# Seven of eleven FFN chunks computed with the tokens stationary, 512 weight columns moving, and the gated values turned on TensorE

## The reference, cut to what matters

```
def swiglu(h, w_in, w_out):                 # h: 256 x 1024
    g, u = jnp.split(h @ w_in, 2, axis=-1)  # w_in: 1024 x 5632, so g and u: 256 x 2816
    return (jax.nn.silu(g) * u) @ w_out     # w_out: 2816 x 1024
```

## Time and profile before

| | us |
|---|---|
| median of 3 runs | 961.66 |
| lowest, highest | 959.19, 961.93 |
| profiled execution, its own time | 958.76 |
| its span in the trace | 957.0 |
| PE busy in the span | 915.8 (96%) |
| PE weight loads | 834.0 (87%) |
| DVE busy | 681.8 (71%) |
| ACT busy | 508.0 (53%) |
| mean granted clock of TensorE | 0.986 of 2.4 GHz |

### The profile page before, as it was taken

One profiled execution on the slowest core, in us unless ns is written; L12 is line 12 of the kernel. 1 busy time (PEld: TensorE's weight loads), 2 busy tenths in 40 slices (PEclk: granted clock), 3 DMA queues, 4 the chain that ended last, 5 costly groups with the idle time before them and its releaser, 6 DMA issues.

```text
span 957.0 us, 14577 instructions
## 1 busy us (share of the span) xinstructions
PE 915.8 (96%) x6039; PEld 834.0 (87%) x6041; DVE 681.8 (71%) x903; ACT 508.0 (53%) x800; POOL 40.6 (4%) x100
## 2 busy tenths in 40 slices
PE   4979999999999999999899999999999999999996
PEld 2879997999999988999789999998987899999974
DVE  5879876887877877998777664466797855555555
ACT  2554545744434456877574443444783744444454
POOL 2101010010000100000001000000000000000000
PEclk9889999999999999999999999999999999999998
DMA  8999772898887955675539655574236665556511
GB/s 336 375 362 323 279 253 100 281 373 304 282 294 269 317 173 176 220 265 176 177 135 363 206 177 179 188 230 141 89 133 220 206 218 192 177 182 237 197 45 44
DMA packets 125763, 212.75 MB, mean 222 GB/s; under 512 B 4753, under 2 KB 93954, under 8 KB 125698
## 3 DMA queue, kind: packets, MB, share of 16 engines
q1 hardware_dynamic: 113362, 164.63, 50.7%
q0 software_dynamic: 12336, 47.20, 14.0%
HBM read 210.75 MB, written 1.06 MB: 221 GB/s over the span
## 4 chain that ended last, share of the span: by engine, by line
PE 84%; DVE 5%; ACT 5%; DMA 4%; issue 1%; SPq 0%; DVEq 0%; ACTq 0%
PE ps L607 24%; PE ps L609 24%; PE ps L608 24%; DMA raw<-in_moba_w_qkv 3%; PE ps L658 2%; PE ps L660 2%; PE ps L666 2%; DMA ada_raw<-in_ada_w 1%; PE ps L885 1%; ACT w_hi L1113 1%; ACT w_hi L1112 1%; DVE w_lo L1562 1%; DVE w_lo L1555 1%; DVE ada_sum L1586 1%; DMA raw<-in_w_up 1%
## 5 line engine op out<-in xcount | busy, mean ns | idle before, releaser
L607 PE MATMUL ps<-h_hi,w_hi 128*128 128x256 f32 x1136 | 322.5, 284 | 0.0
L609 PE MATMUL ps<-h_hi,w_lo 128*128 128x256 f32 x1136 | 321.5, 283 | 0.0
L608 PE MATMUL ps<-h_lo,w_hi 128*128 128x256 f32 x1136 | 321.4, 283 | 0.0
L1555 DVE TENSOR_TENSOR w_lo<-raw,w_hi 128x1024 fp32r<-128x1024 f32 x145 | 177.4, 1223 | 132.8 <-ACT w_hi L1112 132.8
L1112 ACT ACTIVATE w_hi<-raw 128x1024 fp32r<-128x1024 f32 x145 | 153.1, 1056 | 219.1 <-PE ps L609 187.1
L608 PEld LDWEIGHTS ps<-h_lo,w_hi 128*128 128x128 f32 x1136 | 217.9, 192 | 1.3
L607 PEld LDWEIGHTS ps<-h_hi,w_hi 128*128 128x128 f32 x1136 | 217.9, 192 | 1.3
L609 PEld LDWEIGHTS ps<-h_hi,w_lo 128*128 128x128 f32 x1136 | 217.9, 192 | 0.0
L1562 DVE TENSOR_TENSOR w_lo<-raw,w_hi 128x1024 fp32r<-128x1024 f32 x145 | 176.7, 1219 | 0.0
L1113 ACT ACTIVATE w_hi<-raw 128x1024 fp32r<-128x1024 f32 x145 | 151.7, 1046 | 0.0
L607 PE MATMUL ps<-w_hi,o_hi 128*128 128x512 f32 x264 | 105.6, 400 | 1.1 <-DVE w_lo L1562 1.1
(11 more groups left out here) (305 smaller groups left out, 1167.4 us busy)
## 6 DMA issues: line engine op xcount, KB each, us to landing
raw<-in_ffn_w_in SPq DMA_DIRECT2D x40, 1024.0 KB, 5.3
ada_raw<-in_ada_w POOLq DMA_DIRECT2D x31, 1024.0 KB, 6.7
raw<-in_ffn_w_out SPq DMA_DIRECT2D x22, 1024.0 KB, 5.0
raw<-in_w_up SPq DMA_DIRECT2D x16, 1024.0 KB, 5.3
raw<-in_w_down SPq DMA_DIRECT2D x16, 1024.0 KB, 4.9
raw<-in_moba_w_qkv SPq DMA_DIRECT2D x12, 1024.0 KB, 10.3
raw<-in_diff_w_qkv SPq DMA_DIRECT2D x10, 1024.0 KB, 5.1
yg<-in_ada_w POOLq DMA_DIRECT2D x9, 1024.0 KB, 6.2
```

The source lines that it names most:

```text
L607: T.matmul(out_ap, hi_s, hi_m, start=start, stop=False, skip_group_check=True)
L608: T.matmul(out_ap, hi_s, lo_m, start=False, stop=False, skip_group_check=True)
L609: return T.matmul(out_ap, lo_s, hi_m, start=False, stop=stop, skip_group_check=True)
L1555: V.tensor_tensor(w_lo[:, n.place, FRONT], raw[:, n.raw_place, FRONT], w_hi[:, n.place, FRONT].bitcast(F32), ALU.subtract).then_inc(front_ ...
```

## The change

In chunks 2 to 8 of both layers (`by_token`) `gate_up_tokens` takes the place of `gate_up`. The two column slabs are now the two halves of w_in's rows, each with 256 gate and 256 up columns, loaded by `load_two`. A tile of `h` (128 tokens) is stationary, 512 weight columns move, into two PSUM banks (one for each token tile). The silu and the product are made for each token tile (`gated_tile`, `hidden_tile`), PE turns the gated values after the second quarter of `down(c-1)` (`turn_hid`), and the high and low parts are read from PSUM (`turned_hi`, `turned_lo`). The gate bank of layer l is now used for the turned values; in chunks 9 and 10 the gate goes to the bank `FF_FREE`. On ACT the split of n+4 now stands ahead of the silus.

```
...
+                def gate_up_tokens(n, chunks):
+                    pe.wait_ge(hid_ready, chunks)
+                    for s in range(2):
+                        wh, wl = as_halves(w_hi[:, (n + s).place]), as_halves(w_lo[:, (n + s).place])
+                        for t in range(ST):
+                            for k in range(4):
+                                if t == 0 and k % 2 == 0:
+                                    pe.wait_ge((front_lo, slab_lo)[k // 2], n.plus(s + 1))
+                                last = three(ps[:, FF_FIRST[l][t]], h_hi[:, 4 * s + k, tokens(t)],
+                                             h_lo[:, 4 * s + k, tokens(t)], wh[:, k], wl[:, k], s == 0 and k == 0,
+                                             s == 1 and k == 3)
+                            if (s, t) == (1, 0):
+                                last.then_inc(tile_done, 1)
+                        last.then_inc(slab_done, 1)
+
+                def turn_hid(chunk):
+                    pe.wait_ge(tile_hid, turned_chunks(l, chunk))
+                    pe.wait_ge(hid_ready, base + chunk + 1)
+                    for o in range(2):
+                        for t in range(ST):
+                            last = T.transpose(ps[:, FF_GATE[l], o * S + t * P:o * S + (t + 1) * P],
+                                               hid[:, t, o * P:(o + 1) * P], ident[:])
+                    last.then_inc(hid_turned, 1)
...
                     if turns:
                         i = TURN_CHUNKS.index(chunk)
                         pe.wait_ge(ada_lo_ready, i + 1)
                         pe.wait_ge(mod_ready, i + 4)
-                    down(n + 2, base + chunk, (chunk - 1) % 2, reduce_two if turns else None)
+                    def inside(quarter):
+                        if turns:
+                            reduce_two(quarter)
+                        if by_token(chunk) and quarter == 1:
+                            turn_hid(chunk)
+                    down(n + 2, base + chunk, (chunk - 1) % 2, inside)
...
+                def gated_tile(chunk, n, t):
+                    if t == 0:
+                        act.wait_ge(tile_done, turned_chunks(l, chunk))
+                    else:
+                        act.wait_ge(slab_done, n.plus(2))
+                    A.activation(silu_g[:, t], ps[:, FF_FIRST[l][t], 0:256], ACT.Silu).then_inc(tile_silu, 1)
...
                     split_hi(n + 3)
                     if chunk == FF_CHUNKS - 2:
                         gate_hi(2 * l + 1)
-                    gated(n)
-                    split_hi(n + 4)
+                    if by_token(chunk):
+                        split_hi(n + 4)
+                        gated_tile(chunk, n, 0)
+                        gated_tile(chunk, n, 1)
+                    else:
+                        gated(n, FF_GATE[l] if chunk == 1 else FF_FREE[l])
+                        split_hi(n + 4)
                     if l == 0 and chunk in TURN_CHUNKS:
                         i = TURN_CHUNKS.index(chunk)
                         act.wait_ge(ada_acc, summed(ADA_LATER + 5 * i + 4))
                         act.wait_ge(ada_reduced, i + 4)
                         A.activation(ada_hi, ada_sum[:, SLOT_COLS], ACT.Copy).then_inc(ada_hi_ready, 1)
...
                     if l == 0 and chunk in TURN_CHUNKS:
                         i = TURN_CHUNKS.index(chunk)
                         dve.wait_ge(ada_hi_ready, i + 1)
                         V.tensor_tensor(ada_lo, ada_sum[:, SLOT_COLS], ada_hi.bitcast(F32), ALU.subtract)\
                             .then_inc(ada_lo_ready, 1)
                     if last:
                         split_lo(n + 4)
-                    hidden(base + chunk + 1)
+                    if by_token(chunk):
+                        hidden_tile(chunk, n, 0)
+                        hidden_tile(chunk, n, 1)
+                    else:
+                        hidden(base + chunk + 1)
...
```

More of the change, by code:

```diff
@@ L138, in ada_last, with by_token, turned_chunks @@
     return max(i for i in range(m) if ADA[i][3] == ADA[m][3])
+def by_token(chunk):
+    return 2 <= chunk < FF_CHUNKS - 2
+N_BY_TOKEN = sum(map(by_token, range(FF_CHUNKS)))
+def turned_chunks(l, chunk):
+    return N_BY_TOKEN * l + sum(map(by_token, range(chunk + 1)))
 TWO_LOADS = [first + h for first in (FFN[0], ATTN[1], FFN[1]) for h in range(2)]
+TWO_LOADS += [FFN[l] + 3 * chunk - 1 + h for l in range(DEPTH) for chunk in range(FF_CHUNKS) if by_token(chunk)
+              for h in range(2)]
 class Slab:
@@ L377, in build @@
             sem(n) for n in ("silu_ready", "hid_ready", "hid_hi_ready", "hid_lo_ready"))
+        tile_done, tile_silu, tile_hid, hid_turned = (
+            sem(n) for n in ("tile_done", "tile_silu", "tile_hid", "hid_turned"))
         relu_ready = sem("relu_ready")
@@ L442, in load, with load_two @@
                 sp.dma_start(parts(raw[:, n.raw_place]), src).then_inc(slab_loaded[n.raw_place], 16)
-            def load_two(n, w, h, second):
+            def load_two(n, w, h, second, first=0):
                 sp.wait_ge(slab_lo, n.plus(1 - RAW))
                 for g in range(2):
-                    src = w.rearrange("(h k p) n -> p h k n", p=P, k=4)[:, h, :, g * second:g * second + 256]
+                    src = w.rearrange("(h k p) n -> p h k n", p=P, k=4)[:, h, :, first + g * second:first + g * second + 256]
                     sp.dma_start(as_halves(raw[:, n.raw_place])[:, :, g * 256:(g + 1) * 256], src)                        .then_inc(slab_loaded[n.raw_place], 16)
@@ L496, in _ @@
                     n = Slab(FFN[l] + 2 + 3 * j)
-                    load(n, cols(ffn_w_in[l], j * 256 + 256), as_cols)
-                    load(n + 1, cols(ffn_w_in[l], j * 256 + (D_FF + 256)), as_cols)
+                    if by_token(j + 1):
+                        for h in range(2):
+                            load_two(n + h, ffn_w_in[l], h, D_FF, j * 256 + 256)
+                    else:
+                        load(n, cols(ffn_w_in[l], j * 256 + 256), as_cols)
+                        load(n + 1, cols(ffn_w_in[l], j * 256 + (D_FF + 256)), as_cols)
                     load(n + 2, rows(ffn_w_out[l], j), as_rows)
@@ L963, in gate_up @@
                     pe.wait_ge(hid_ready, chunks)
-                    col_slab(n, FF_GATE[l])
+                    col_slab(n, FF_FREE[l])
                     col_slab(n + 1, FF_UP[l])
+                def gate_up_tokens(n, chunks):
[20 more added lines that the diff above has]
+                    last.then_inc(hid_turned, 1)
                 base = FF_CHUNKS * l
@@ L982, in _ @@
                     n = Slab(FFN[l] + 3 * chunk - 1)
-                    gate_up(n, base + chunk)
+                    if by_token(chunk):
+                        gate_up_tokens(n, base + chunk)
+                    else:
+                        gate_up(n, base + chunk)
                     if chunk == FF_CHUNKS - 2:
                         pe.wait_ge(mod_ready, 7)
-                        spread_row((FF_FREE[l], MISC), 2 * l + 1)
+                        pe.wait_ge(hid_lo_ready, base + chunk)
+                        spread_row((FF_GATE[l], MISC), 2 * l + 1)
                     turns = l == 0 and chunk in TURN_CHUNKS
@@ L1340, in _, with gated @@
                 split_hi(n + 2)
-                def gated(n):
+                def gated(n, bank):
                     act.wait_ge(slab_done, n.plus(1))
-                    A.activation(silu_g[:], ps[:, FF_GATE[l]].rearrange("p (o s) -> p o s", o=2), ACT.Silu)\
+                    A.activation(silu_g[:], ps[:, bank].rearrange("p (o s) -> p o s", o=2), ACT.Silu)\
                         .then_inc(silu_ready, 1)
@@ L1353, in gated_tokens, with turned_hi @@
                     A.activation(silu_g[:, t], ps[:, FF_FIRST[l][t], 0:256], ACT.Silu).then_inc(silu_ready, 1)
+                def gated_tile(chunk, n, t):
[4 more added lines that the diff above has]
+                    A.activation(silu_g[:, t], ps[:, FF_FIRST[l][t], 0:256], ACT.Silu).then_inc(tile_silu, 1)
+                def turned_hi(chunk, parts):
+                    act.wait_ge(hid_turned, turned_chunks(l, chunk))
+                    A.activation(hidden_parts(parts)[0], ps[:, FF_GATE[l]].rearrange("p (o s) -> p o s", o=2), ACT.Copy)\
+                        .then_inc(hid_hi_ready, 1)
                 def hidden_hi(chunk, parts):
@@ L1380, in _ @@
                         split_hi(n + 5)
-                    hidden_hi(base + chunk + 1, chunk % 2)
+                    if by_token(chunk):
+                        turned_hi(chunk, chunk % 2)
+                    else:
+                        hidden_hi(base + chunk + 1, chunk % 2)
                     if chunk == FF_CHUNKS - 1:
@@ L1922, in hidden @@
                 def hidden(chunk):
-                    dve.wait_ge(silu_ready, chunk + l + 1)
+                    at = chunk - base
+                    dve.wait_ge(silu_ready, chunk + l + 1 - turned_chunks(l, at - 1))
                     dve.wait_ge(slab_done, n.plus(2))
```

(23 more changed lines are left out.)

## The result

The changed kernel takes 968.42 us (median of 4 runs, 968.09 to 972.42); the kernel before takes 960.42 us (median of 4, 957.59 to 961.93). The ratio is 1.0099, 95% interval 1.0076 to 1.0122: slower by about 1%. The forecast was 971 us in a range of 964 to 976.5 us. The profiled executions are 968.41 us (span 966.6 us) against 958.76 us (span 957.0 us), 9.6 us apart.

The account below looks back on a forecast made before the run. PE was taken to bound the kernel; -8.0 + 6.3 + 9.0 + 3.2 = +10.5 us gave 969.3 us from the profiled execution, 972.2 us from the runs' median. The forecast was 971 us between them, range 964 to 976.5 us.

Parts of the forecast that it names:

- The column slabs: `gate_up` in 14 chunks: 48 steps of 512 columns replace 96 of 256, 0.57 us less each, -8.0 us.
- Rival B: 512-column steps in the new `gate_up` take 213 ns, slabs gain 9.8 us more, sum +0.7 us; chance 3%.
- The turns: Four transposes on PE inside `down` in each of 14 chunks, with a slower step behind them: +6.3 us.
- The wait for `ada_lo_ready`: PE stands still 3.0 us before `down` in chunks 3, 5 and 8 of layer 0: +9.0 us.
- The clock: PE at half clock after its breaks in layer 0, two falls taken of none to three: +3.2 us.
- rival C: Each of layer 0's three breaks brings twice the half-clock stretch, costing 9.6 us, sum +17 us; chance 7%.
- The loads, ACT and DVE: Slabs loaded in two half-size DMAs, and tile-wise silus and products beside a bounding PE: no cost.
- The sum: Whole kernel: -8.0 + 6.3 + 9.0 + 3.2 = +10.5 us on the profiled execution of 958.76 us.
- Rival A: No PE stall before `down` in chunks 3, 5 and 8 of layer 0, sum -1.7 us; chance 6%.

Follow-up runs that it names:

- e3: Kernel e1 with each turn made twice, 8 transposes in place of 4: 963.20 us, ratio 1.0039 to the kernel before.
- e1: The changed kernel with ACT writing `ada_hi` of layer 0's chunks 3, 5 and 8 ahead of the two tile silus: 955.99 us, ratio 0.9968 to the kernel before.
- e4: The kernel before, with ACT writing `ada_hi` of layer 0's chunks 3, 5 and 8 only after `gate_up` has ended: 968.64 us, ratio 1.0100.
- e2: The changed kernel with 11 matmuls of zeros on PE while it would wait for `ada_lo_ready`: 967.01 us, ratio 1.0078 to the kernel before.
- e7: The changed kernel with no edit, profiled once more in another execution: 968.21 us in one run.
- e6: Kernel e1 with the turn ahead of `down`, where PE must wait for the second tile's silu and product: 976.18 us in one run.

## Why the prediction was right, step by step

- **The column slabs** were put at -8.0 us. `gate_up` fell from 11.51 to 10.87 us, 0.64 us in 14 chunks, -9.0 us. The distance in the new loop is 0.2265 us, a little below the 0.2279 of `down`. The Trainium skill's formula for the isolated gap ("TensorE: Matmul & The Clock Gate", "Back-to-back issue gap") would put this term at -1.7 us by the estimate in the prediction; these are streams of matmuls, each with its own weight load, and they gained 12 to 13 ns a pair, so the runs do not agree with it. Rival B, 213 ns a step, is out by the same 0.2265 us.
- **The turns** were put at +6.3 us. `down` grew from 5.47 to 5.92 us, 0.45 us in 14 chunks, +6.3 us; e3 confirms the part that lies in the transposes.
- **The wait for `ada_lo_ready`** was put at 3.0 us three times. It is 2.83 us and a first step about 0.12 us longer, 8.8 us in all. The sum put PE's new start 2.89 us behind D, the moment at which `down` would start; it came at 2.83, as the silu began at D + 0.19 us instead of D + 0.27. e1 takes it away, and e4 makes it without the change.
- **The clock** was put at two falls of 1.6 us. It was two, of 1.46 us by e2. The mechanism and the price of one fall were right; that it was two is luck within the stated bounds: e7 shows one long fall, e4 one short. The doubled stretch of rival C does occur, at one of nine breaks, but not at each of three as that rival had it.
- **The loads, ACT and DVE** were put at nothing. No wait of PE but the three for `ada_lo_ready` shows from 190 to 330 us of the changed kernel, and e1, which keeps the halved loads and the tile-wise work, has none in either FFN.
- **The sum** was +10.5 us on the profiled execution and came to +9.6 in the spans: 1.0 of slabs, 0.2 of the wait and 0.3 of the clock less, and 0.4 of other stages more; 0.2 us is not assigned. The middle of 971 us was 2.6 us high mainly because I had set the kernel before between its profiled 958.76 us and its median of 961.66; its later runs came out near 959 us.
- **Rival A**, no stall, is what e1 builds: it was put at -1.7 us and measures -2.6 us in the FFNs (-1.37 and -1.22; FFN 1 of e1 is 168.25 us).

## What to carry to other kernels

When an instruction is split so that its last part waits for something later, look at what stands behind it on the same engine, and who waits for that: here a side task of 1 us, written after the silu, became the thing that TensorE waited for. Put work without a late input ahead of the wait. A break in the bounding engine costs its length; with TensorE it cost here in four cases of nine another 1.5 to 3 us at half clock. To price one stage, compare the distance between two marks around it: the whole time also holds what the clock did elsewhere.

## What the runs showed of the hardware

- At full clock float32r matmuls with a 128x128 weight load each come every 119.9 ns for 256 moving columns and every 226.5 to 227.9 ns for 512 (kernels before and after): one step of 512 saves 12 to 13 ns over two of 256. At half clock the step of 512 is 0.43 us.
- Four float32 transposes of 128x128 cost 0.35 us (e1), and the step behind them is 0.08 to 0.1 us longer; eight cost 0.80 us and the same restart (e3).
- Breaks of PE of 1.0 us, 14 of them (e6), brought no half clock. Of nine breaks of 2.5 to 2.7 us idle (changed kernel twice, e4) four brought it, three for 3.4 us and one for 6.8 us. With 11 matmuls of zeros in the break and 0.3 us of idle (e2) none of three did.
- The same code can be granted another clock in another execution: from 25.0 to 45.5 us, ahead of every edit, the mean was 0.50 to 0.51 in the profiles of e1 and e6 and 0.78 to 0.83 in the others.
